# First stage of a hybrid block by channels, without the norm's factor for blocks 0 to 2

## The reference

```python
h  = concatenate([meta, x])                    # 16 + 1024 rows
hn = rms_norm(h, mix_norm_g)                   # h * rsqrt(mean(h*h) + eps) * g
proj = hn @ w_in                               # 1024 x 6656
rq, rk, rv, rg, sq, sk, sv, gr, gs = split(proj)
y_ret = rms_norm(retention(rq, rk, rv), ret_norm_g) * silu(rg)
y_swa = sliding_window_attention(rms_norm(sq), rms_norm(sk), sv, sinks)
h = h + (sigmoid(gr) * (y_ret @ w_ret) + sigmoid(gs) * (y_swa @ w_swa)) @ w_out
h = h + square(relu(rms_norm(h, mlp_norm_g) @ w_up)) @ w_down
return h without the meta rows
```

## Time and profile before

| | |
|---|---|
| median of 3 runs | 1614.77 us (1614.22 to 1615.44) |
| the profiled execution | 1615.03 us, its span 1613.1 us |
| TensorE busy | 1603.3 us, 99% of the span |
| VectorE, ScalarE, GpSimd busy | 1038.1, 769.6, 425.7 us |
| granted TensorE clock | 1.00 |
| first product of the first stage, meta rows, second stage | 9.34, 59.62, 63.25 us |

### The profile page before, as it was taken

How to read it: one execution, slowest core, us unless ns; L and a number is a source line. 1 busy time by engine, 2 the same in 40 slices (tenths; PEclk the granted TensorE clock), 3 DMA queues, 4 the chain that set the end, 5 groups by cost and what they waited for, 6 DMA issues and landing times.

```text
span 1613.1 us, 22668 instructions
## 1 busy us (share of the span) xinstructions
PE 1603.3 (99%) x7984; PEld 1340.3 (83%) x7984; DVE 1038.1 (64%) x1977; ACT 769.6 (48%) x1567; POOL 425.7 (26%) x611
## 2 busy tenths in 40 slices
PE   8999999999999999999999999999999999999999
PEld 6888888888888888888888888888888888888887
DVE  6775556655657787766554338866665656766675
ACT  6533334544547777762122126655555544444442
POOL 1001010221238898874211000122112222100000
PEclk9999999999999999999999999999999999999999
DMA  8323231645436566668553223354444389633452
GB/s 282 125 97 117 98 124 66 239 149 190 163 110 159 158 176 167 159 159 267 167 187 111 66 78 118 126 174 151 144 144 155 120 316 358 240 96 98 153 180 92
DMA packets 128815, 253.31 MB, mean 157 GB/s; under 512 B 14928, under 2 KB 50176, under 8 KB 128704
## 3 DMA queue, kind: packets, MB, share of 16 engines
q1 hardware_dynamic: 82656, 124.81, 24.8%
q0 software_dynamic: 45904, 126.93, 23.5%
q10 hardware_dynamic: 144, 0.13, 0.0%
HBM read 157.05 MB, written 69.47 MB: 140 GB/s over the span
## 4 chain that ended last, share of the span: by engine, by line
PE 93%; DMA 2%; DVE 2%; POOL 1%; ACT 1%; issue 0%; SPq 0%; DVEq 0%; ACTq 0%
PE bank L1089 29%; PE bank L1094 28%; PE bank L1093 28%; PE bank L1375 2%; PE bank L1407 1%; PE bank L1389 1%; DMA RT<-YA 1%; DMA XCH<-in_x_ch 0%; POOL PR L966 0%; PE bank L1132 0%; PE bank L1507 0%; PE bank L1293 0%; PE bank L1424 0%; PE bank L1457 0%; DVE WL L2177 0%; PE bank L1411 0%
## 5 line engine op out<-in xcount | busy, mean ns | idle before, releaser
L1089 PE MATMUL bank<-WH,ADH 128*128 128x512 f32 x448 | 174.3, 389 | 0.0
L1093 PE MATMUL bank<-WH,ADL 128*128 128x512 f32 x448 | 174.3, 389 | 0.0
L1094 PE MATMUL bank<-WL,ADH 128*128 128x512 f32 x448 | 174.3, 389 | 0.0
L1089 PE MATMUL bank<-HN,WH 128*128 128x512 f32 x384 | 152.9, 398 | 0.1
L966 POOL TENSOR_SCALAR PR<-PR,RC 128x272 f32<-128x272 f32 (+1 forms) x128 | 139.3, 1228 | 47.4 <-DVE RC L2672 47.2
L2103 ACT CAST ADH<-ARAW 128x512 fp32r<-128x512 f32 x112 | 69.5, 621 | 169.9 <-PE bank L1094 156.7
L1094 PE MATMUL bank<-HN,WH 128*128 128x512 f32 x384 | 150.2, 391 | 0.0
L1093 PE MATMUL bank<-HN,WL 128*128 128x512 f32 x384 | 150.1, 391 | 0.0
L2926 DVE TENSOR_TENSOR ADL<-ARAW,ADH 128x512 fp32r<-128x512 f32 x112 | 77.5, 692 | 97.1 <-ACT ADH L2103 97.1
L1089 PE MATMUL bank<-SOPH,WH 128*128 128x512 f32 x256 | 99.8, 390 | 0.0
L1093 PE MATMUL bank<-SOPH,WL 128*128 128x512 f32 x256 | 99.6, 389 | 0.0
(11 more groups left out here) (356 smaller groups left out, 4200.6 us busy)
## 6 DMA issues: line engine op xcount, KB each, us to landing
ARAW<-uop SPq DMA_DIRECT2D x112, 256.0 KB, 3.1
uop<-US POOLq DMA_DIRECT2D x64, 256.0 KB, 2.8
WRAW<-in_w_up SPq DMA_DIRECT2D x15, 1024.0 KB, 6.3
PW<-PR SPq DMA_DIRECT2D x56, 272.0 KB, 3.0
RAW<-in_w_in SPq DMA_DIRECT2D x58, 256.0 KB, 4.1
gates<-TB POOLq DMA_DIRECT2D x48, 256.0 KB, 2.7
uop<-UA POOLq DMA_DIRECT2D x48, 256.0 KB, 3.2
proj<-SA POOLq DMA_DIRECT2D x36, 256.0 KB, 2.5
```

The lines of the kernel that those rows point to most:

```text
L1089: mm = pe.matmul(bank, ahi, bhi, start=first, stop=False, skip_group_check=onto)
L1093: pe.matmul(bank, alo, bhi, start=False, stop=False, skip_group_check=onto)
L1094: return pe.matmul(bank, ahi, blo, start=False, stop=last, skip_group_check=onto)
```

## The change

Blocks 0 to 2 enter the first stage as x times g by channels, without the token's factor; the factor is applied when their bank is evicted, as ScalarE's scale. ScalarE makes the high part with g as its scale (`hi_xg`), VectorE x times g minus that (`lo_xg`), into `XGH` and `XGL`. Blocks 0 and 1 take turns, two channel tiles each, so that a weight tile serves both. All eight blocks are now scaled from channels to `SR` in the order 3, 4, 5, 6, 7, 0, 1, 2 (`SEQ`), blocks 0 to 2 only for the second stage. The square sums run in the order 3, 4, 0, 5, 1, 2, 6, 7, meta (`STAT`), and stand elsewhere in ScalarE's list; VectorE's reciprocals (`invert`) stand apart from the diagonals (`factors`). g's columns are loaded from ScalarE's queue, the raw channels lead SyncE's. SyncE's parts PX to PZ stay behind the last channel load, which waits for the fifth scaling; PY waits also for block 2's products, since `XGH` lies there. The factor row p stands behind these steps of TensorE: `ROWS`.

```diff
+SEQ = (3, 4, 5, 6, 7, 0, 1, 2)
+STAT = (3, 4, 0, 5, 1, 2, 6, 7, NB)
 # SyncE
-            sp.dma_start(XR[:, 0, :], x[0:P, :]).then_inc(x0_full, 16)
-            sp.dma_start(GCH[:, :], g_ch).then_inc(gc_full, 16)
-            sp.dma_start(IDN[:, :], c_ident).then_inc(id_full, 16)
+            LATE_XG = {1: (1, 0), 3: (0, 1), 4: (1, 1)}    # behind weight tile k
+            load_xg(0, 0)
             load_slab(0, w_cols(w_in, 0))
+            sp.dma_start(XCH[:, 2, :, :], x_ch[2]).then_inc(xc_full[2], 16)
+            for p in range(NB):
+                if p < 3:
+                    sp.wait_ge(hn_lo, max(XG_AT[p, 0], XG_AT[p, 1]))
+                else:
+                    sp.wait_ge(xs_rdy, 2 * (p - 2))
+                sp.dma_start(XCH[:, p % 3, :, :], x_ch[SEQ[p]]).then_inc(xc_full[p % 3], 16)
             sp.dma_start(GBC[0:META, :], g_mix[0:META, :]).then_inc(g_full, 16)
 # GpSimd: load_x(i) loads block STAT[i], from i = 4 on after ss_rdy >= i - 3
+            pool.wait_ge(w_ready, 5)
+            load_x(0)
+            pool.wait_ge(hn_hi, NXG)
+            for i in range(1, 4):
+                load_x(i)
...
+            load_x(4)
+            load_x(5)
             store_rq(0)
+            load_x(6)
+            store_rq(1)
             load_x(7)
+            store_rq(2)
             load_x(8)
 # TensorE
+            keep_warm(4)
+            for pair in range(KT // 2):
+                for b in range(2):
+                    for k in (2 * pair, 2 * pair + 1):
+                        first_step(b, k)
+            ROWS = {(2, 1): 0, (3, 0): 1, (3, 5): 2, (4, 3): 3, (5, 1): 4, (5, 6): 5, (6, 4): 6, (7, 2): 7}
+            for b in range(2, NB):
...
+                for k in range(KT):
+                    first_step(b, k)
+                    if (b, k) in ROWS:
+                        factors_row(ROWS[b, k])
+                    if (b, k) == (6, 6):
+                        transpose_meta()
 # ScalarE
+            def hi_xg(b, u):
...
+                for k in range(4 * u, 4 * u + 4):
+                    hi = act.activation(XGH[:, b, k, :], XCH[:, b, k, :], ACT.Copy, scale=GCH[:, k:k + 1])
+            def evict_first(b):
...
+                if b < FIRST:
+                    act.wait_ge(rstd_rdy, STAT_AT[b] + 1)
+                    act.activation(TB[:, b % 2, :], first_bank(b)[:, :], ACT.Copy, scale=RSTD[:, b:b + 1]).then_inc(a_free, 1)
...
+            act.dma_start(GCH[:, :], g_ch).then_inc(gc_full, 16)
...  # hi_xg and split_hi in turn, then:
+            square_x(0); square_x(1); hi_x(3); square_x(2); evict_first(0); square_x(3); hi_x(4)
+            square_x(4); evict_first(1); square_x(5); evict_first(2); hi_x(5); square_x(6); evict_first(3)
+            hi_x(6); square_x(7); evict_first(4); hi_x(7); square_x(8); evict_first(5); hi_x(0); hi_meta()
+            hi_x(1); evict_first(6)   # then st_hi(0, 0, 0..3), hi_x(2), evict_first(7)
 # VectorE
+            def lo_xg(b, u):
+                dve.wait_ge(hn_hi, XG_AT[b, u])
+                for k in range(4 * u, 4 * u + 4):
+                    lo = dve.scalar_tensor_tensor(out=XGL[:, b, k, :], in0=XCH[:, b, k, :], scalar=GCH[:, k:k + 1],
+                                                  in1=XGH[:, b, k, :].bitcast(F32), op0=ALU.mult, op1=ALU.subtract)
...  # lo_xg and split_lo in turn, then:
+            invert(3)
+            factors(3)
+            for p in range(NB):
+                scale_x(p)
+                if p == 2:
+                    invert(2)
+                if p < 4:
+                    invert(SEQ[p + 1])
+                if p < NB - 1:
+                    factors(SEQ[p + 1])
+                lo_x(SEQ[p])
+                if p < 2:
+                    invert(p)
+                elif p == 4:
+                    invert(NB)
+                    norm_meta()
+                elif p == 6:
+                    for k in range(4):
+                        st_lo(0, 0, k)
+            for b in range(4, NB):
+                first_sum(b)
```

More of the change, by code:

```diff
@@ L57 @@
 START = 1
+FIRST = 3
+SEQ = (3, 4, 5, 6, 7, 0, 1, 2)
+AT = {b: p for p, b in enumerate(SEQ)}
+STAT = (3, 4, 0, 5, 1, 2, 6, 7, NB)
+STAT_AT = {b: p for p, b in enumerate(STAT)}
+MAKE_META = 5
 ORD = (0, 1, 4, 2, 5, 3, 6, 7)
@@ L582, in build @@
         pst_a, pst_b, PSA0, PSB0 = out_done, h1_ld, 16 * 12 * NSG, 16 * 4 * NSG
-        rt_full, RT0 = x_full, 32
-        kv_full, KV0 = x_full, 64
+        rt_full, RT0 = x_full, [48, 32, 32, 32]
+        kv_full, KV0 = x_full, [RT0[i] + 32 for i in range(4)]
         GS0, CF0, MU0 = 4, 48, 64
@@ L1165, in st_product @@
                     bank = st_bank(g, t, f)
+                    if g == 0 and t == 0 and f == 2:
+                        pe.wait_ge(hn_lo, lo_at(2, 1))
                     for k in range(4):
@@ L1185, in tokens @@
                 return lambda k: (pair[0][:, k, b * P:(b + 1) * P], pair[1][:, k, b * P:(b + 1) * P])
[L1187 to L1200, removed]
             def keep_warm(count):
@@ L1206, in keep_warm, with xg_block @@
                     pe.matmul(B[1][:, 0:2 * P], WARM[:, 0:P], WARM[:, 0:2 * P], start=True, stop=True)
[L1208 to L1221, removed]
-                for k in range(KT):
[L1223 to L1227, removed]
+            def xg_block(b):
+                return lambda k: (XGH[:, b, k, :], XGL[:, b, k, :])
@@ L1243, in _, with first_step @@
[L1243 to L1249, removed]
-                    dense_a("M", b, B[b % 2], 0, hn_block(b), 0, False, True, loop=False,
-                            middle=lambda: transpose_x(NB))
-            pe.wait_ge(hn_lo, 2 * NB)
+            def first_step(b, k):
+                if k % 4 == 0:
+                    pe.wait_ge(hn_lo, XG_AT[b, k // 4] if b < FIRST else lo_at(b, k // 4))
+                mm = step("M", first_bank(b), k, 0, (xg_block if b < FIRST else hn_block)(b), 0, b == 0, b == NB - 1)
+                if k == KT - 1:
+                    mm.then_inc(a_full, 1)
@@ L2225, in _, with factors, norm_meta @@
-            norm_x(0)
-            split_lo(0, 0)
-            lo_x(0, (0,))
-            for k in range(1, 4):
-                split_lo(0, k)
-            lo_x(0, (1,))
+            def factors(b):
+                dve.wait_ge(rstd_rdy, STAT_AT[b] + 1)
+                dve.tensor_scalar(DG[:, AT[b] % 2, :], IDN[:, :], RSTD[:, b:b + 1], None, ALU.mult).then_inc(xn_rdy, 1)
+            def norm_meta():
+                dve.wait_ge(rstd_rdy, STAT_AT[NB] + 1)
+                dve.wait_ge(g_full, 16)
+                dve.scalar_tensor_tensor(out=ST[0:META, :], in0=XR[0:META, STAT_AT[NB] % 4, :], scalar=RSTD[0:META, NB:NB + 1],
+                                         in1=GBC[0:META, :], op0=ALU.mult, op1=ALU.mult).then_inc(xn_rdy, 1)
@@ new lines, in scale_x @@
+            def scale_x(p):
+                dve.wait_ge(xt_full, row_at(p))
+                dve.wait_ge(xc_full[p % 3], 16 * (p // 3 + 2))
+                for u in range(2):
+                    for i in range(4):
+                        k = 4 * u + i
+                        part = dve.scalar_tensor_tensor(out=x_cols(SEQ[p], u)[:, i, :], in0=XCH[:, p % 3, k, :],
+                                                        scalar=GCH[:, k:k + 1], in1=B[6 + p % 2][:, 0:P], op0=ALU.mult,
+                                                        op1=ALU.mult)
+                    part.then_inc(xs_rdy, 1)
```

302 lines of the change are left out of this document (150 added, 152 removed).

## The result

The changed kernel takes 1622.55 us (median of four executions, 1621.48 to 1625.06) beside 1614.74 for the kernel before: a ratio of 1.0049, interval 1.0033 to 1.0065. So it is slower, by 7.8 us, where 1617.8 was forecast and 1621.0 was the upper end. The profiled execution took 1622.90, its span is 1621.1.

What follows compares the result with a forecast made beforehand. TensorE bounds the kernel (93% of the chain). 1615.03 + 1.5 (waits outweigh the earlier start) + 1.5 (block 6's rows late) = 1618.0, less 0.26 to the median: 1617.8 us; range from 1613.7, with 0.7 to spare, to 1621.0.

Steps and rivals of the forecast that it cites:

- Block 3 at 23.7: Start: block 3's first product at 23.7 us instead of 30.27, 6.6 us won, with block 4 ready at 23.9.
- S: Time of block 3's first product on TensorE, forecast at 23.7 us.
- The loop from block 3 on: Blocks 3 to 7: factor rows hang on VectorE and ScalarE, TensorE waits 7.4 us, net +1.5 us at the meta rows.
- M: Start of the meta rows on TensorE, forecast at 61.1 us, 37.4 us behind block 3's first product; 59.62 before.
- Block 6's rows: Rows of x for block 6's square, asked for at about 26.4, take 8.2 us and land late: +1.5 us.
- Rival 2: Rows come late: block 6's rows take 11.3 us, block 4's wait is 7.3 us, run 1621.0; chance 0.22.
- Behind the meta rows: Second stage: VectorE has four more first sums, no cost forecast, up to 1 us if it slips.
- Four scaled copies: Start: ScalarE's four scaled 128x128 copies cost 0.95 us, within 0.55 to 1.4.
- Rival 1: From block 3 on: diagonals are ready before their rows, the start's gain stays, run 1608.8; chance 0.11.
- row 3: Factor row behind block 4's fourth step, due 8.65 us after block 3's start; forecast to wait 2.65 for block 6's diagonal.
- The last quarter hidden: Last of SP's four quarter loads lands at 60.8, wanted about 2.7 us after the meta rows start: no cost.
- Rival 4: TensorE's clock falls to 1.2 GHz in block 4's wait, net 1.2 us more, run 1619.0; chance 0.07.

Runs made afterwards that it cites:

- with the rows: Changed kernel with GpSimd's loads of x rows for blocks 3 and 4 asked for sooner: 1621.40 us, ratio 1.0040 to the kernel before.
- with the clock: Changed kernel with those two row loads sooner and seven warm-up products in place of four: 1621.87 us, ratio 1.0040 to the kernel before.

## Why the prediction was wrong

By its own steps, in the profiled execution: forecast 1618.0, measured 1622.90, a difference of 4.9.

- **Block 3 at 23.7: the step that failed, +3.56.** "Just in time" was not: at 27.26 block 3 is past the 26 that the prediction itself named as a failed start. The failed step is the price and the place of the rows of x. Block 4's were to be asked for at 15.5, take 5.15 us, the one such load in the chain, and have block 3 ready 3.2 us later, at 23.9. They were asked for at 16.6 (1.1 later), took 7.9 (2.75 more), and block 3 started 2.77 us behind them (0.4 less): 3.4 of the 3.56, and the rest lies between its 23.9 and its 23.7. The DMA engines were busy 92%, as before (91%); the 8.2 of the earlier trace rows would have been right. The first factor row, which waits for block 3's rows (7.7 us), was given no wait and stood 1.17. Two more misses are hidden behind these rows: the first product came at 7.40, 0.6 late, and the first seven products cost 1.5 more at the lower level of the clock, which the prediction had looked for only behind a new wait in block 4, and not at the start, where the change takes away the transposes that had kept TensorE at work up to 9.34. Without them the factor row would only have waited longer, as it did with seven warm-up products alone. The experiments give back 1.9 with the rows and 0.6 more with the clock; 1.0 of the 3.56 is left (S 24.73), and the first product comes 0.5 late there (7.31).
- **The loop from block 3 on: right, mis-sized by +1.07.** Waits of 2.65, 1.6 and 3.5 were forecast at just these three rows, released by just these engines; 3.25, 1.23 and 3.15 came, 7.63 for 7.75; that the sum fits so well is in part luck, since each is off by 0.35 to 0.6, and not the same way. (The prediction speaks of 7.4, which is 37.4 less 30.0; its three waits add up to 7.75, and its walk leaves 29.65 for TensorE's work.) M - S is 38.47 for 37.4 because TensorE takes 30.84 beside the waits. About 0.7 of what lies above 30.0 is the price of standing: each of the three waits costs 0.24 more than its idle time, 0.16 as above and 0.08 at the row behind it, which takes 0.22 to the next start (39.50 to 39.72) for 0.13 to 0.14 without a wait (28.07 to 28.20).
- **Block 6's rows, +1.5 forecast: not there.** Its rows had landed by 35.9, and its square (37.41) follows ScalarE's copies without a pause. Rival 2, which had them late there, falls with it; that its 1621.0 lies nearer to the result than the forecast is luck. Rows were late, but at the start.
- **Behind the meta rows, none forecast: +1.9.** The span ends 1555.4 us after M for 1553.5. By the starts of the same products in both traces three waits make 1.7 of it: 0.44 for a first sum of VectorE at 86, which the prediction had as its "up to 1 us if it slips", 0.38 at a DMA of the retention stage (511), 0.90 at a weight's rest at 917. 0.2 stays open. 0.13 less lies around the span.
- **Four scaled copies: 1.28 us** for 0.95, inside the bounds of 0.55 to 1.4; one takes 0.386. (3.9 and 0.95 make 4.85, not the 4.95 of the prediction.) The Trainium skill (ScalarE: Activation LUTs, What ACT_TABLE_LOAD costs) gave 0.39 by its 93 ns for such an operand: the trace agrees, and the nearest rows had it 0.08 too low.
- **Rival 1, the loop hides: decided at row 3, as it said.** Block 6's diagonal was made at 39.11, the row was due at 36.25. But its price was too high: with waits of 0.8 us left the run is at 1613.7, not 1608.8, since S stays at 24.7 and most of the lead at M is lost behind it.
- **The last quarter hidden:** yes at M = 65.73; no, by 1.5 us, at 57.37.
- **Rival 4, the clock, had 0.07:** the mechanism is real and was the largest price in the experiments (over 4 us). In the changed kernel's profiled execution no wait brought it; the slow first products are hidden as said above.

3.56 + 1.07 - 1.5 + 1.9 - 0.13 = 4.9.

## What to carry to other kernels

A gain at the start of a chain is worth what its latest input leaves of it: price every load that the earlier start needs at a load under the same traffic (7.7 and 7.9 us here), not at the one that happened to lie on the old chain (5.15). Where a statistic moves from "a block ahead" to "just in time", write down each in-order list that it passes; here one order of ScalarE's list, with the loads of its rows, was worth 2.8 us of waits and one 64 KB load 2.3. And where an edit takes filler work away from TensorE, or makes it wait some 3 us, count the products behind at half pitch, and look at pitch as well as at the column of the granted clock.

## What the runs showed of the hardware

- Of eleven waits of TensorE of 2.8 us or more behind the start (2.80 to 5.87), in the profiled executions, the granted clock fell to 0.50 in or behind nine and stayed at 1.00 behind the two of the changed kernel; behind waits of up to 2.17 between S and M it stayed. What decides is open.
- The column of the granted clock read 1.00 while the first products of the changed kernel ran at a pitch of 0.43; behind long waits in other kernels the same pitch stood beside 0.50.
- Loads of 512 KB of x took 5.2 to 9.7 us from issue to landing within one stage.
